# Three of the four left-half loads of x move to ScalarE's queue, and the first weights and the norm factors change places behind the first block

## What is computed

```python
h = concatenate([meta, x])
h = h + token_mixer(rmsnorm(h, norm_mix), w_in, w_uv, w_out)
hn = rmsnorm(h, norm_ffn)
h = h + peer(hn, peer_wq, peer_subkeys, peer_u, peer_v)
return rmsnorm(h, norm_final)[:, N_META:]
```

## Time and profile before

| | us |
|---|---|
| median of 3 runs | 1694.59 (1693.92 to 1695.63) |
| the profiled execution, time | 1696.27 |
| the profiled execution, span from first to last instruction | 1694.3 |
| TensorE busy | 1675.1 |
| VectorE, GpSimd, ScalarE busy | 1099.0, 923.4, 576.5 |
| granted clock of TensorE, mean | 0.997 |

### The profile page before, as it was taken

How to read it: one execution, slowest core, us unless ns; L and a number is a source line. 1 busy time by engine, 2 the same in 40 slices (tenths; PEclk the granted TensorE clock), 3 DMA queues, 4 the chain that set the end, 5 groups by cost and what they waited for, 6 DMA issues and landing times.

```text
span 1694.3 us, 23275 instructions
## 1 busy us (share of the span) xinstructions
PE 1675.1 (99%) x7756; PEld 1376.9 (81%) x7756; DVE 1099.0 (65%) x2944; ACT 576.5 (34%) x910; POOL 923.4 (55%) x883
## 2 busy tenths in 40 slices
PE   9999999999999999999999999999999999999998
PEld 7867767888888888888888888888888888888886
DVE  4269967457888844444444444435788888888887
ACT  5443225243323222222222222224333333333333
POOL 3654311014442057777777777753777677767710
PEclk9999999999999999999999999999999999999999
DMA  6322141045778444444456444555999999999991
GB/s 180 108 64 76 36 112 44 26 174 178 275 247 281 149 144 148 149 143 145 142 193 205 145 142 144 149 160 211 388 390 365 376 367 365 372 375 364 364 341 53
DMA packets 183361, 351.26 MB, mean 207 GB/s; under 512 B 35728, under 2 KB 119056, under 8 KB 183120
## 3 DMA queue, kind: packets, MB, share of 16 engines
q1 hardware_dynamic: 118512, 255.70, 45.0%
q0 software_dynamic: 34816, 67.41, 11.1%
q10 hardware_dynamic: 29952, 27.28, 4.8%
HBM read 289.27 MB, written 61.02 MB: 207 GB/s over the span
## 4 chain that ended last, share of the span: by engine, by line
PE 81%; issue 2%; DVE 2%; POOL 1%; ACT 1%; DVEq 0%; POOLq 0%
PE psum L293 26%; PE psum L295 26%; PE psum L294 26%; PE psum L1154 1%; PE psum L1162 1%; POOL ts_lo_wq L1689 1%; PE psum L1176 1%; PE psum L1851 1%; PE psum L1205 1%; DVE att_masked L1415 0%; POOL cand L2100 0%; POOL ts_lo_u L1689 0%; DVE wlo_out L333 0%; PE psum L1190 0%; PE psum L1218 0%
## 5 line engine op out<-in xcount | busy, mean ns | idle before, releaser
L2502 POOL DMA_INDIRECT gate_map<-gate_total,gate_at x384 | 403.5, 1051 | 200.8 <-DVE same_expert L2197 110.1
L293 PE MATMUL psum<-x_hi,ts_hi_u 128*128 128x512 f32 x1024 | 399.4, 390 | 1.9 <-POOL ts_lo_u L1689 1.2
L295 PE MATMUL psum<-x_hi,ts_lo_u 128*128 128x512 f32 x1024 | 398.8, 389 | 0.0
L294 PE MATMUL psum<-x_lo,ts_hi_u 128*128 128x512 f32 x1024 | 398.8, 389 | 0.0
L1689 DVE TENSOR_TENSOR ts_lo_u<-ts_raw_u,ts_hi_u 128x1024 fp32r<-128x1024 f32 x116 | 142.2, 1226 | 336.6 <-ACT ts_hi_u L1684 336.6
L295 PE MATMUL psum<-v_hi,c_lo 128*128 128x512 f32 x768 | 299.1, 389 | 0.0
L293 PE MATMUL psum<-v_hi,c_hi 128*128 128x512 f32 x768 | 299.1, 389 | 0.0
L294 PE MATMUL psum<-v_lo,c_hi 128*128 128x512 f32 x768 | 299.0, 389 | 0.0
L1684 ACT ACTIVATE ts_hi_u<-ts_raw_u 128x1024 fp32r<-128x1024 f32 x128 | 135.4, 1058 | 394.6 <-PE psum L295 394.6
L2397 ACT ACTIVATE v_hi<-v_raw 128x1024 fp32r<-128x1024 f32 x128 | 135.8, 1061 | 314.0 <-PE psum L295 314.0
L293 PEld LDWEIGHTS psum<-x_hi,ts_hi_u 128*128 128x128 f32 x1024 | 192.3, 188 | 42.1 <-POOL ts_lo_u L1689 1.4
(11 more groups left out here) (278 smaller groups left out, 2300.9 us busy)
## 6 DMA issues: line engine op xcount, KB each, us to landing
ts_raw_u<-in_peer_u SPq DMA_DIRECT2D x128, 512.0 KB, 3.6
v_raw<-in_peer_v SPq DMA_DIRECT2D x128, 512.0 KB, 6.0
gate_map<-zeros SPq DMA_DIRECT2D x32, 768.0 KB, 6.2
act_in<-up_acts SPq DMA_DIRECT2D x128, 192.0 KB, 5.5
gate_in<-gate_map SPq DMA_DIRECT2D x128, 192.0 KB, 6.5
up_acts<-ut_out_u ACTq DMA_DIRECT2D x104, 192.0 KB, 1.9
raw_in<-in_w_in SPq DMA_DIRECT2D x56, 256.0 KB, 2.8
ts_raw_wq<-in_peer_wq SPq DMA_DIRECT2D x16, 512.0 KB, 5.1
```

The costliest lines, as they stand in the source:

```text
L293: nc.tensor.matmul(out, l_hi, r_hi, start=first, stop=False)
L294: nc.tensor.matmul(out, l_hi, r_lo, start=False, stop=False)
L295: return nc.tensor.matmul(out, l_lo, r_hi, start=False, stop=last)
L2502: nc.gpsimd.indirect_dma_start(gate_cells, bass.IndirectOffsetOnAxis(places["gate_at"][:, b, j:j + 1], 0), dn.total[:, b, j:j + 1], None). ...
```

## The change

Behind `ident`, SyncE now issues left half 0, weight unit 0 and then `gcol`; weight unit 1 and the right halves follow as before. Left halves 1 to 3 are issued by ScalarE on its own queue, behind its wait for `ident` and ahead of its first square root. No byte is added or left out, and all semaphores stay the same.

```diff
+    def load_left(eng, b):
+        eng.dma_start(mixed[:, b, 0:HALF], io["x"][b * P:(b + 1) * P, 0:HALF]).then_inc(left_in[b], 16)
+
     with nc.Block() as block:
         @block.sync
         def _(sp):
             sp.dma_start(ident[:], io["ident"]).then_inc(ident_in, 16)
+            load_left(sp, 0)
+            load_unit(sp, ws, 0, in_unit(io, 0))
             sp.dma_start(gcol[:], io["norm_mix"]).then_inc(g_in, 16)
-            for b in range(NB):
-                if b == NB - 1:
-                    load_unit(sp, ws, 0, in_unit(io, 0))
-                sp.dma_start(mixed[:, b, 0:HALF], io["x"][b * P:(b + 1) * P, 0:HALF]).then_inc(left_in[b], 16)
             load_unit(sp, ws, 1, in_unit(io, 1))
...
             act.wait_ge(ident_in, 16)
+            for b in range(1, NB):
+                load_left(act, b)
             load_root_table(nc, sb, c, "mix", ident)
             act.wait_ge(g_in, 16)
```

## The result

The changed kernel is slower by a quarter of a per cent, and 1.1 us beyond the top of my range.

A forecast was written before the change was run, and what follows sets the result against it. TensorE bounds the kernel, with the fourth left half's landing as its clock. 7.5 transfers give 11.4, less 0.46 is 10.94 against 8.67: +2.27 on the median 1694.59 makes 1696.9 us; range 1694.0 to 1698.4.

The forecast's parts named there:

- The edits that I put at nothing: Start of the kernel: gcol and first weights moved, ScalarE's table load behind its issues, later weights' landing; each claimed worth nothing.
- the 0.46 us of the earlier start: Head of SyncE's queue: left half 0 issued at 1.19 instead of 1.65, so bulk transfers start 0.46 us sooner.
- the landing: Fourth left half, before the first product: lands at 10.94 against 8.67, +2.27 us.
- my upper bound of 2.6: Fourth left half's landing strictly behind all transfers issued earlier or with it: eight transfers, shift at most +2.6 us.
- rival (a): First loads: ScalarE's transfers alternate fairly with SyncE's from the start; +1.2 us, 1695.8; chance 0.20.
- work already issued goes first: DMA queues at the first loads: earlier issued work goes first, then queues alternate; taken as 7.5 transfers, landing +2.27 us.
- rival (c): TensorE's waits ahead of blocks two to four: clock falls, costing 1.0 to 1.7 us; together +3.3 to +4.0; chance 0.12.
- the sign I gave for (c): Before the first product: warming transposes of twice the length behind 9 us.
- the sum of waits that I forecast: TensorE ahead of line 587: waits three times for x, in sum over 2 us.
- No wait before the barrier is there to swallow it: TensorE between first product and barrier: argument against rival (d), shift swallowed further on, 1694.6, chance 0.05.

## Why the prediction was right and wrong

*The cause was right, its price was not.* The left halves compete with the second weights and right halves that SyncE issues sooner: hold those back and the loss is gone, put the left halves back on one queue in their old order and it is gone. The fourth left half sets the pace of the projection, TensorE waits three times ahead of it, 3.4 us in sum, left 2 and right 0 land together (10.11 and 10.30), and the shift goes through the barrier. The edits that I put at nothing (`gcol`, the first weights, ScalarE's late table load, the later weights) cost nothing; the 0.46 us of the earlier start came out as 0.35. Two terms of the sum failed: the landing, which was mis-sized, and the clock, which the sum put at nothing.

*The landing was mis-sized: +3.23, not +2.27, and beyond my upper bound of 2.6.* I had counted transfers, 7.5 of them, on the assumption that what is issued first goes first and that a landing comes when its bytes have moved. Neither holds. The queues take turns from about 4.2 us, 381 packets to 349, even with transfers issued later. The Trainium skill states it so, DMA: Bandwidth & Descriptors, section "Queues, rings and completion order": each DMA engine goes round its queues packet by packet; the trace agrees. My rival (a) was this mechanism, and yet its price of +1.2 was further off, because fair turns are only the middle of the story. The landing waits for the last of sixteen parts, and these spread over 2.9 us in one trace of the changed kernel and 4.2 in the other, instead of 1.7; with the old head beside the same second queue it was 1.45, and left 3 came 1.2 us sooner. A store that moved no packet for over a microsecond led me to "work already issued goes first"; what held that store back, these runs don't show. Its 347 packets to none don't agree with two queues that interleave, as I wrote; the 87 to 86 do, and now the 381 to 349.

*The clock's fall was no rival to the forecast: it came on top of it.* I set rival (c) beside the forecast with 0.12, and named as its condition that the second and third left halves each come a microsecond behind TensorE. The waits came as 0.86, 2.10 and 0.42, and with them the sign I gave for (c), longer warming transposes (1.94 and, in the second execution, 2.76 us for 1.47). In the first execution the way from the landing to the first product is 0.88 us longer than before, and filling the waits took 0.85 of it away, less than the 1.0 to 1.7 that I allowed; in the second it is 1.60 longer (12.95 to 16.32). Had I added even 1.0 to +2.27, the forecast would have been 1697.9 and the chances of slower near even. Yet the sum of waits that I forecast, over 2 us, did not make the fall certain: in the same place 2.7, 2.6 and 2.3 us of waits lost no clock (the same order on SyncE, only the right halves held, the third weights sooner), while 3.4 and 4.3 us did. The term hangs on the landing, and the landing was the first step to fail.

*"No wait before the barrier is there to swallow it"* holds for a loss, as the 3.84 of 4.11 show. For a gain it is false: 0.5 to 0.6 us earlier, TensorE meets GpSimd's rotated block at 39.1, and 0.2 to 0.5 us stay there. And the list of waits that I read has one more ahead of the barrier, 2.6 us for `ident` at line 608, which I passed over. The change leaves it as it was, but in the two kernels where ScalarE issues from 0.74 it grew to 4.0 and 3.4, and little or nothing was left of the earlier landing.

*The median moved by more than the trace.* 4.7 us between the medians stand beside 3.6 between the profiled executions. Two things scatter: the first 17 us (4.1 and 5.9 us lost in two executions), and the fall of the earlier trace rows, which also the changed kernel's first trace has, 4 us later, and its second has not. It is worth about 1.7 us: the kernel with one queue and the new head lacks it, and its span is 2.1 us shorter than before's with a barrier only 0.35 earlier. Recorded falls are not the whole of the difference. Each execution comes with its mean granted clock, and no traced execution with a mean of 0.999 has such a fall. The four of the changed kernel's twelve with that mean took 1696.77, 1698.85, 1699.23 and 1699.24 us, those of the kernel before 1693.5 to 1695.7 in all comparisons; three of the four are 4 us slower without a fall. A later landing, or a clock that rises late, does not show in that mean; which of them it is in these executions was not traced. Open, too, is why one of sixteen parts comes so late: the packets don't show their engine.

## What to carry to other kernels

A second issuing queue is not a faster path for what is wanted first: here it let later work in beside it, and the last part of the wanted load came latest of all. Order the loads by need in one queue, and if a second one is used, hold the first one's later loads until the wanted ones are through. Where a change makes TensorE wait several times in a row, give the clock a term in the sum, on top of the waits, and not a place among the rivals.

## What the runs showed of the hardware

- A queue's last few packets can cost more than the many before: two kernels had moved equally many of ScalarE's packets by 7.5 us (384 and 380 of 432), and the landing came at 8.04 in one and at 10.20 in the other.
- A load of 64 KB feels a second queue as well: `ident` held TensorE to 4.0 instead of 2.6 when the other queue's loads were issued beside it from 0.74.
- Work that nobody reads kept the clock: with 38 warming transposes ahead of the three waits in place of 6, the granted clock did not fall before the first product.
- A clock that has not risen yet is missing from the views: with the old head and the left halves on ScalarE they print 1.00 from the start, while four transposes take 1.06 to 1.12 us up to 11.9, where they take 0.60 at the high level.
